# Second layer norm from differences to a pivot, gathered during the last feed-forward block

## What is computed

```python
def layer_norm(x, g, b):
    mu = xf.mean(-1, keepdims=True)
    var = jnp.square(xf - mu).mean(-1, keepdims=True)
    return ((xf - mu) * lax.rsqrt(var + LN_EPS) * g + b)
...
    h = layer_norm(ALPHA * x + mix, ln1_g, ln1_b)
    u = jnp.square(jax.nn.relu(jnp.einsum('bsd,df->bsf', h, w_ff1) + b_ff1))
    f = jnp.einsum('bsf,fd->bsd', u, w_ff2) + b_ff2
    return layer_norm(ALPHA * h + f, ln2_g, ln2_b)
```

## Time and profile before

| | |
|---|---|
| median of 3 runs | 1890.46 us (1890.34 to 1891.09) |
| the profiled execution | 1891.25 us |
| its span, first to last instruction | 1889.65 us |
| TensorE matmul / VectorE / ScalarE / GpSimd busy | 1826.7 / 911.7 / 773.2 / 103.7 us |
| granted TensorE clock, mean | 0.984 of full |
| last feed-forward matmul ends, last store issued | about 1849.8 us, 1878.15 us |

### The profile page before, as it was taken

The page is one execution under the profiler, slowest core; times in us unless marked ns, Lnnn a source line. Parts: engine busy times, 40 slices in busy tenths (PEclk is TensorE's granted clock), DMA queues, the critical chain, the costliest instruction groups (busy, mean ns, idle before and its releaser), DMA issues.

```text
span 1889.7 us, 33735 instructions
## 1 busy us (share of the span) xinstructions
PE 1826.7 (97%) x12750; PEld 1766.2 (93%) x12750; DVE 911.7 (48%) x1197; ACT 773.2 (41%) x1063; POOL 103.7 (5%) x208
## 2 busy tenths in 40 slices
PE   7999999999999999999599999999999999999993
PEld 7999999988888889999499999999999999999992
DVE  5555543365555545644664444444444444444444
ACT  5444543455555553332344332443234332343322
POOL 0000000101111111100000000000000000000000
PEclk9999999999999999999799999999999999999996
DMA  8555565676666656655347576666667666666631
GB/s 258 145 155 149 158 176 162 201 271 236 213 211 247 203 200 208 214 170 172 102 159 240 181 239 206 216 207 213 222 199 236 209 216 205 214 211 210 220 102 56
DMA packets 270911, 369.04 MB, mean 195 GB/s; under 512 B 11921, under 2 KB 264529, under 8 KB 267905
## 3 DMA queue, kind: packets, MB, share of 16 engines
q1 hardware_dynamic: 250368, 249.17, 43.5%
q0 software_dynamic: 9088, 106.90, 14.5%
q10 hardware_dynamic: 11392, 12.13, 1.9%
HBM read 356.02 MB, written 70.71 MB: 226 GB/s over the span
## 4 chain that ended last, share of the span: by engine, by line
PE 95%; DVE 3%; ACT 1%; DMA 0%; issue 0%; DVEq 0%; SPq 0%; ACTq 0%
PE psM L960 29%; PE psM L961 29%; PE psM L962 29%; PE psM L1008 1%; PE psO L1055 1%; PE psT L1034 1%; PE psM L1021 1%; PE psO L1068 1%; DVE s_r L885 1%; DVE s_r L894 1%; PE psT L980 0%; PE psO L1070 0%; PE psO L1065 0%; PE psM L1012 0%; PE psT L1149 0%; PE psO L1083 0%
## 5 line engine op out<-in xcount | busy, mean ns | idle before, releaser
L670 DVE TENSOR_TENSOR s_wlo<-s_raw,s_whi 128x1024 fp32r<-128x1024 f32 x468 | 573.7, 1227 | 730.7 <-ACT s_whi L414 725.5
L414 ACT ACTIVATE s_whi<-s_raw 128x1024 fp32r<-128x1024 f32 x468 | 495.1, 1058 | 900.0 <-PE psM L962 876.4
L960 PE MATMUL psM<-s_xhi,s_whi 128*128 128x320 f32 x1248 | 392.2, 314 | 10.6 <-DVE s_xlo L675 9.9
L961 PE MATMUL psM<-s_xlo,s_whi 128*128 128x320 f32 x1248 | 386.7, 310 | 0.0
L962 PE MATMUL psM<-s_xhi,s_wlo 128*128 128x320 f32 x1248 | 386.7, 310 | 0.0
L960 PE MATMUL psM<-s_hhi,s_whi 128*128 128x320 f32 x1024 | 317.8, 310 | 9.0 <-DVE s_hlo L880 8.7
L961 PE MATMUL psM<-s_hlo,s_whi 128*128 128x320 f32 x1024 | 317.5, 310 | 0.0
L962 PE MATMUL psM<-s_hhi,s_wlo 128*128 128x320 f32 x1024 | 317.4, 310 | 0.0
L962 PE MATMUL psM<-s_uhi,s_wlo 128*128 128x320 f32 x1024 | 316.4, 309 | 0.0
L961 PE MATMUL psM<-s_ulo,s_whi 128*128 128x320 f32 x1024 | 316.4, 309 | 0.0
L960 PE MATMUL psM<-s_uhi,s_whi 128*128 128x320 f32 x1024 | 316.4, 309 | 0.0
(11 more groups left out here) (160 smaller groups left out, 1593.0 us busy)
## 6 DMA issues: line engine op xcount, KB each, us to landing
s_raw<-in_w_ff_dram SPq DMA_DIRECT2D x256, 512.0 KB, 3.7
s_raw<-in_w_in_dram SPq DMA_DIRECT2D x156, 512.0 KB, 4.1
s_kvbuf<-in_kT_b_dram POOLq DMA_DIRECT2D x8, 2448.0 KB, 9.1
s_kvbuf<-in_v_b_dram POOLq DMA_DIRECT2D x8, 2304.0 KB, 8.3
s_raw<-in_w_out_dram SPq DMA_DIRECT2D x32, 512.0 KB, 3.5
out_b_s_dram<-in_cache_b_kv_dram POOLq DMA_DIRECT2D x16, 1008.0 KB, 6.1
s_raw<-in_w_branch_a_dram SPq DMA_DIRECT2D x16, 512.0 KB, 3.5
gates_scratch<-s_gstage ACTq DMA_DIRECT2D x16, 320.0 KB, 3.3
```

The source lines that it names most:

```text
L414: act.activation(whi[:, slot], raw[:, slot], ACT.Copy).then_inc(hi_done, 1)
L670: dve.tensor_tensor(wlo[:, slot], raw[:, slot], whi[:, slot].bitcast(F32), ALU.subtract).then_inc(lo_done, 1)
L960: pe.matmul(out, wh, hi[:, t0 + k], start=first and k == 0, stop=False)
L961: pe.matmul(out, wh, lo[:, t0 + k], start=False, stop=False)
```

## The change

It replaces the second layer norm and the last block's eight `w_ff2` groups; the first layer norm stays.

- **Pivot.** When groups 0 to 3 are added (tiles 0 to 7 of `r`), VectorE folds the two rows of sums into one, TensorE sums it behind the first quarter of group 4, and ScalarE copies twice that mean to SBUF: the pivot, the mean of the first half of the features. VectorE subtracts it from all 16 tiles during group 4. By construction the first eight tiles then add up to zero.
- **Gathering.** During groups 5 and 6 ScalarE squares the tiles that are finished and VectorE adds squares and tiles up; in group 7, behind its third quarter, TensorE sums both rows of tiles 0 to 13. Tiles 14 and 15 follow behind the last matmul. Out of the mean of differences and the mean of their squares come the rest of the mean and the variance.
- **Apply.** VectorE takes the rest of the mean off tiles 0 to 3, GpSimd off 4 to 15, four at a time, from a copy in SBUF. VectorE multiplies all tiles, with the reciprocal in PSUM; the affine step of a tile is ScalarE's (10 tiles), GpSimd's (5) or VectorE's (1), by the string `Y_BY`.
- **Stores.** SyncE issues eight stores of two tiles, in order, each behind its two tiles, and waits for them; GpSimd no longer does.

The groups of the last block are written out instead of looped, on TensorE, ScalarE and VectorE. The core of the diff:

```diff
--- before.py
+++ after.py
+        B3 = 3 * C_BLK + C_FF + 32
+        Y_BY = "APAPAAAPAAAPAAPD"
+        MULS = ((0, 2), (2, 4), (4, 8), (8, 12), (12, 16))
+        def y_ready(t):
+            by = Y_BY[t]
+            return {"A": y_act, "P": y_pool, "D": y_dve}[by], Y_BY[:t + 1].count(by)
+        def muls_for(t):
+            return 1 + [lo <= t < hi for lo, hi in MULS].index(True)
...
+            yv = o["yT"].rearrange("(t p) n -> p t n", p=P)
+            for k in range(8):
+                sp.wait_ge(*y_ready(2 * k))
+                sp.wait_ge(*y_ready(2 * k + 1))
+                sp.dma_start(yv[:, 2 * k:2 * k + 2], r[:, 2 * k:2 * k + 2]).then_inc(y_out, 16)
+            sp.wait_ge(y_out, 16 * 8)
...
-            pool.wait_ge(y_out, 16 * 4)
+            pool.wait_ge(delta_in, 1)
+            for p in range(1, 4):
+                part = r[:, 4 * p:4 * p + 4]
+                pool.tensor_tensor(part, part, lnx[:, 1:2].broadcast_to([P, 4, NTOK]), ALU.subtract).then_inc(less_p, 1)
+            for t in range(16):
+                if Y_BY[t] == "P":
+                    pool.wait_ge(mul_d, muls_for(t))
+                    pool.tensor_scalar(r[:, t], r[:, t], ln2g[:, t:t + 1], ln2b[:, t:t + 1], ALU.mult, ALU.add).then_inc(y_pool, 1)
...
-                    if li == 0:
-                        act.activation(hhi[:, 4 * p:4 * p + 4], r[:, 4 * p:4 * p + 4], ACT.Copy).then_inc(h_hi, 1)
-                    else:
-                        act.dma_start(o["yT"].rearrange("(t p) n -> p t n", p=P)[:, 4 * p:4 * p + 4],
-                                      r[:, 4 * p:4 * p + 4]).then_inc(y_out, 16)
+                    act.activation(hhi[:, 4 * p:4 * p + 4], r[:, 4 * p:4 * p + 4], ACT.Copy).then_inc(h_hi, 1)
...
-            with act.Fori(0, 7) as q:
+            def square_pair(g):
+                act.wait_ge(*sum_group(g))
+                act.activation({4: xres[:, 0], 5: xres[:, 1], 6: t2[:, 0]}[g], r[:, 2 * g:2 * g + 2], ACT.Square).then_inc(sq_early, 1)
+            for g in range(7):
                 for j in range(4):
-                    split(q + (3 * 16 + C_FF // 4 + 9), j)
-            layer_norm(1, ln2g, ln2b)
+                    split(3 * 16 + C_FF // 4 + 9 + g, j)
+                    if g == 4 and j == 1:
+                        act.wait_ge(piv_sum, 1)
+                        act.activation(piv, psO[:, 0, 0:NTOK], ACT.Copy, scale=2.0).then_inc(pivoted, 1)
+                    if g == 5 and j == 0:
+                        for p in range(2):
+                            act.wait_ge(off_pivot, 3 + p)
+                            act.activation(gt8[:, 4 * p:4 * p + 4], r[:, 4 * p:4 * p + 4], ACT.Square).then_inc(sq_early, 1)
+                        square_pair(4)
+                    if g == 6 and j == 0:
+                        square_pair(5)
+            square_pair(6)
+            act.activation(eps[:, 1:2], eps[:, 0:1], ACT.Sqrt)
+            for t in (14, 15):
+                act.wait_ge(tail_d, t - 13)
+                act.activation(t2[:, 1, t - 14], r[:, t], ACT.Square).then_inc(tail_sq, 1)
+            act.wait_ge(stat_d, 1)
+            act.activation(delta, psO[:, 0, 0:NTOK], ACT.Copy).then_inc(delta_in, 1)
+            act.wait_ge(delta_in, 1)
+            act.activation(dsq, delta, ACT.Square).then_inc(dsq_in, 1)
+            act.wait_ge(var_in, 1)
+            act.activation(std, lnrow[:, 2], ACT.Sqrt, bias=eps[:, 0:1]).then_inc(root_in, 1)
+            for t in range(16):
+                if Y_BY[t] == "A":
+                    act.wait_ge(mul_d, muls_for(t))
+                    act.activation(r[:, t], r[:, t], ACT.Identity, bias=ln2b[:, t:t + 1], scale=ln2g[:, t:t + 1]).then_inc(y_act, 1)
...
+            def take_pivot():
+                dve.wait_ge(pivoted, 1)
+                for p in (2, 3, 0, 1):
+                    part = r[:, 4 * p:4 * p + 4]
+                    dve.tensor_tensor(part, part, lnx[:, 0:1].broadcast_to([P, 4, NTOK]), ALU.subtract).then_inc(off_pivot, 1)
+            def sum_squares(step, out, more):
+                dve.tensor_tensor(out, out, more, ALU.add).then_inc(sq_sum, 1)
+                dve.wait_ge(sq_sum, step)
+            for g in range(7):
+                for j in range(4):
+                    split(3 * 16 + C_FF // 4 + 9 + g, j)
+                    if g == 4 and j == 1:
+                        take_pivot()
+                    if g == 5 and j == 2:
+                        dve.wait_ge(sq_early, 2)
+                        sum_squares(1, gt8[:, 0:4], gt8[:, 4:8])
+                        sum_squares(2, gt8[:, 0:2], gt8[:, 2:4])
+                        dve.wait_ge(sq_early, 3)
+                        sum_squares(3, gt8[:, 0:2], xres[:, 0])
+                    if g == 6 and j == 2:
+                        dve.wait_ge(sq_early, 4)
+                        sum_squares(4, gt8[:, 0:2], xres[:, 1])
+                dve.wait_ge(chunk_done, B3 + 4 * g + 4)
+                pair = r[:, 2 * g:2 * g + 2]
+                if g == 4:
+                    dve.wait_ge(off_pivot, 4)
+                dve.tensor_tensor(pair, pair, psM[(g + 1) % 2][:, :, 0:NTOK], ALU.add).then_inc(evac[(g + 1) % 2], 1)
+                if g < 4:
+                    add_sum(pair, sum_group(g), g + 11)
+                    if g == 3:
+                        dve.wait_ge(summed, 14)
+                        dve.tensor_tensor(lnrow[:, 2], lnrow[:, 0], lnrow[:, 1], ALU.add).then_inc(folded, 1)
+                elif g == 5:
+                    dve.wait_ge(*sum_group(5))
+                    dve.tensor_tensor(t1[:], r[:, 8:10], pair, ALU.add).then_inc(d_sum, 1)
+                elif g == 6:
+                    dve.wait_ge(*sum_group(6))
+                    dve.wait_ge(d_sum, 1)
+                    dve.tensor_tensor(t1[:], t1[:], pair, ALU.add).then_inc(d_sum, 1)
+            dve.wait_ge(d_sum, 2)
+            dve.tensor_tensor(lnrow[:, 0], t1[:, 0], t1[:, 1], ALU.add).then_inc(part_sums, 1)
+            dve.wait_ge(sq_early, 5)
+            sum_squares(5, gt8[:, 0:2], t2[:, 0])
+            dve.tensor_tensor(lnrow[:, 1], gt8[:, 0], gt8[:, 1], ALU.add).then_inc(part_sums, 1)
+            dve.wait_ge(chunk_done, B3 + 32)
+            for t in (14, 15):
+                dve.tensor_tensor(r[:, t], r[:, t], psM[0][:, t - 14, 0:NTOK], ALU.add).then_inc(tail_d, 1)
+            shift = psO[:, 0:1, 0:NTOK].broadcast_to([P, 2, NTOK])
+            dve.wait_ge(delta_in, 1)
+            dve.tensor_tensor(r[:, 0:2], r[:, 0:2], shift, ALU.subtract).then_inc(less_d, 1)
+            dve.wait_ge(stat_sq, 1)
+            dve.wait_ge(dsq_in, 1)
+            dve.tensor_tensor(lnrow[:, 2], psO[:, 1, 0:NTOK], dsq, ALU.subtract).then_inc(var_in, 1)
+            dve.tensor_tensor(r[:, 2:4], r[:, 2:4], shift, ALU.subtract).then_inc(less_d, 1)
+            dve.wait_ge(root_in, 1)
+            dve.reciprocal(psT[:, 0, 0:NTOK], std).then_inc(rstd_in, 1)
+            dve.wait_ge(rstd_in, 1)
+            for k, (lo, hi) in enumerate(MULS):
+                if k < 2:
+                    dve.wait_ge(less_d, k + 1)
+                else:
+                    dve.wait_ge(less_p, k - 1)
+                part = r[:, lo:hi]
+                dve.tensor_tensor(part, part, psT[:, 0:1, 0:NTOK].broadcast_to([P, hi - lo, NTOK]), ALU.mult).then_inc(mul_d, 1)
+            for t in range(16):
+                if Y_BY[t] == "D":
+                    dve.wait_ge(mul_d, muls_for(t))
+                    dve.tensor_scalar(r[:, t], r[:, t], ln2g[:, t:t + 1], ln2b[:, t:t + 1], ALU.mult, ALU.add).then_inc(y_dve, 1)
...
-            layer_norm(1)
+            up_groups(3)
+            def row_sum(out, row, start, stop):
+                return pe.matmul(out, onesD[:], row, start=start, stop=stop)
+            mean_d, mean_sq = psO[:, 0, 0:NTOK], psO[:, 1, 0:NTOK]
+            for g in range(8):
+                par = (g + 1) % 2
+                pe.wait_ge(evac[par], 24 + (E_FF + 8 + g % 2) // 2 + g // 2)
+                for j in range(4):
+                    pe.wait_ge(u_lo, 24 + 2 * j + 2)
+                    chunk(B3 + 4 * g + j, j, psM[par], uhi, ulo, 4 * j, j == 0, j == 3)
+                    if g == 4 and j == 0:
+                        pe.wait_ge(folded, 1)
+                        row_sum(mean_d, lnrow[:, 2], True, True).then_inc(piv_sum, 1)
+                    if g == 7 and j == 2:
+                        pe.wait_ge(part_sums, 2)
+                        row_sum(mean_d, lnrow[:, 0], True, False)
+                        row_sum(mean_sq, lnrow[:, 1], True, False)
+            for t in (14, 15):
+                pe.wait_ge(tail_d, t - 13)
+                mm = row_sum(mean_d, r[:, t], False, t == 15)
+            mm.then_inc(stat_d, 1)
+            for t in (14, 15):
+                pe.wait_ge(tail_sq, t - 13)
+                mm = row_sum(mean_sq, t2[:, 1, t - 14], False, t == 15)
+            mm.then_inc(stat_sq, 1)
```

(25 more changed lines are left out.)

## The result

The changed kernel takes **1876.6 us** (median of 4 runs, 1876.4 to 1878.1), the kernel before 1890.67 in the same comparison: ratio 0.9927, interval 0.991 to 0.9944. It is 14.1 us faster, where 8.5 were forecast, and lies just under the range, 1877.4 to 1885.6. The sign and the mechanism of the tail were right; a term that the forecast set to zero was worth more than 6 us.

What follows compares the result with a forecast made beforehand. TensorE was taken to bound the kernel up to the last matmul, then a 31.05 us serial tail. 31.05 - 19.6 (new tail) - 2.9 (added TensorE work) = 8.5 us saved: 1890.46 to 1882.0, range 1877.4 to 1885.6.

Steps and rivals of the forecast that it cites:

- The 8.3 us behind the landing: From the last store's landing at 1881.35 to the span's end at 1889.65; forecast unchanged, within 1 us either way.
- the zero: Start of the tail: the start of VectorE's last add, released by TensorE, at 1849.87 us in the kernel before.
- The third stretch: From the stores' last byte to the span's end, 8.7 us before and 2.1 after; its saving was not forecast.
- TensorE's added work: Ahead of the tail: a 1.1 us wait in group 4 plus three row sums of 0.6; cost 2.9 us, at most 4.2.
- The cover for the early work: Pivot subtractions, squares and sums before the tail lie beside TensorE's work and cost nothing; some 8 us of room remain.
- GpSimd's subtraction: In the tail, each of three 1280-element subtractions on GpSimd takes 2.89 us, counted by elements read; done at 10.9.
- The stores wait for tile 1: SyncE's first store waits for GpSimd's tile 1, issued at 11.45; 0.95 and 7.2 us of transfers end the tail at 19.6.
- The price of an issue: Each of SyncE's eight store issues takes 0.38 us, as ScalarE's do; all issued by 14.25.
- The quick GpSimd: Rival: GpSimd's tail subtractions take 1.44 us each, saving 12.1 us, time 1878.4; chance 0.16.
- the slow one: Rival: GpSimd's subtractions hold back all stores; slower by over 0.2% if each exceeds 7.0 us; chance 0.03.
- x: Duration of one of GpSimd's three tail subtractions; forecast from about 2.2 to 3.6 us.
- The clock: Rival: TensorE's clock falls to half behind the 1.1 us gap in group 4, losing 2.85 us, time 1884.9; chance 0.12.

Runs made afterwards that it cites:

- e2: The kernel before with one edit: SyncE waits for the four final stores instead of GpSimd; 1883.14 us, ratio to before 0.9964.
- e1: The changed kernel, but GpSimd waits for the eight final stores instead of SyncE; 1883.06 us.
- e3: The changed kernel with TensorE's pivot row sum behind the second quarter of group 4 instead of the first; 1874.89 us.
- e4: The changed kernel with GpSimd's five affine tiles taken away, ScalarE doing tiles 0 to 11 and VectorE 12 to 15; 1873.33 us.
- e5: As e4, with GpSimd's three subtractions also moved to VectorE, so GpSimd does nothing in the tail; 1875.39 us.

## Why the prediction was wrong, step by step

- **The step that failed: "The 8.3 us behind the landing I leave as they are: SyncE instead of GpSimd waits for the stores, and nothing is queued behind that wait; no row prices it, and I keep 1 us either way."** Something was queued behind that wait: the drain at the end of GpSimd's program, 7.745 us. And a row priced it, that of line 52 in the trace of before, so "no row shows" was wrong too: the chain of before and its timelines show no such instruction, and the forecast took the gap in these views for a gap in the trace. The waits on SyncE's queue do name the line, with 64.4 us that end with the span (from 1825.2 to 1889.6):

```profile
SPq L52 <- PEq L52: 64.4, 1, 64.4
```

What the runs showed in its place: the wait alone saves 7.1 us (e2) and giving it back costs 6.5 (e1). With the row read, the end would have come about 0.4 us behind the last landing or 7.75 behind GpSimd's last tile, whichever is later. By the forecast's own sum that tile ends 13.4 us behind the zero (10.9 and five of 0.5), so the drain ends at 21.15, 1.6 behind the last byte, and the span 0.2 later. The third stretch would have been 7 us shorter, and the forecast about 1875.

- **TensorE's added work, 2.9 us.** The sum is right, 2.9, in part by luck: by e3 the wait cost 1.33 (1.1 forecast) and a row sum 0.54 (0.6), and the two errors cancel.
- **The cover for the early work.** Right: behind the pivot TensorE shows no other gap up to the tail; its next wait, 0.6 us, is for VectorE's tail add.
- **GpSimd's subtraction, 2.89 by elements read.** Right: 8.61 for three, 2.9 one (2896 ns by its group). The Trainium skill's GPSIMD Engine Reference, section Performance versus the Vector engine, gave an estimate of 2.8; the trace agrees, and twice VectorE's 1.48 for that shape is the ratio that the page states. The affine tile was undersized, 0.62 us (3.10 for five) for 0.5.
- **The stores wait for tile 1, then 7.2 us of transfers.** Right: the first store 11.8 us behind the zero (11.45), and 7.4 us without a break. e4 shows the wait: without it the first store came 3.2 us earlier. The tail to the last byte was 20.1 for 19.6, 0.5 too small. The price of an issue was wrong and cost nothing: the eight took 5.93 us, 0.74 each and not 0.38, so they were through 17.7 us behind the zero and not at 14.25, still ahead of the last byte.
- **The quick GpSimd and the slow one** did not happen: x was 2.9. Nor did the two engines hold each other up: VectorE's multiplies of 1280 elements took 1482 ns on average beside GpSimd, and 1487 in e5, where GpSimd does nothing. **The clock** did not fall behind the gap. It was 1.00 there and fell only within the tail, after the last row sum, as the windows of the changed kernel show:

```profile
1797.00:1798.00 1.00, 0.00 (x0) 0.00 (x0) 0.96 (x2) 0.90 (x1) 0.00 (x0) 1.00 0.67 197
1798.00:1799.00 1.00, 0.93 (x4) 0.78 (x5) 0.83 (x2) 0.15 (x1) 0.00 (x0) 1.00 0.92 325
...
1858.00:1858.50 0.50, 0.00 (x0) 0.00 (x0) 0.50 (x1) 0.00 (x0) 0.50 (x2) 0.67 0.00 0
```

- **The range.** Its low end took the quick GpSimd and 1 us at the program's end. Both ends of the unknown 8.3 us should have stood in it: where no row seems to price a stretch, the stretch itself is what can be gained.

## What to carry to other kernels

Read the end of the program too: list each engine's last instructions, those that count as not busy included, and see which engine is last and what it does behind its last wait. The wait for the final stores belongs on an engine whose end is short, here SyncE, and GpSimd's last work should end by at least its drain ahead of the last landing, if another engine can take the rest for less than the drain costs (in e5, with all of it on VectorE, it could not). When stores go out in order and the transfers fill the time, the first one matters most, so its tiles go to the engine that is free first, not to the slowest.

## What the runs showed of the hardware

GpSimd's drain at the end of its program lasts 7.7 to 7.8 us from whatever it did last: behind a wait for stores (7.745 and 7.749, before and e1), in the middle of the last block with its transfers done (7.745 in e2 and e5), behind subtractions (7.7 in e4) and behind affine tiles (7.8 in the changed kernel). SyncE's drain takes 7 ns behind its wait for the stores, 128 ns in e1, where it follows the last issue. In the changed kernel the drains of ScalarE, VectorE and TensorE end within about 0.1 us of their engine's last instruction. Why GpSimd's is so long, and whether a program can shorten it, was not tried.
